# A two-block transformer kernel: parts of the branch outputs by blocks, one branch piece moved ahead of the last turn, merges moved ahead of the output weights' splits

## The reference, cut to what matters

```python
def hybrid_layer(x, c_act, ...):
    ...
    proj = h @ w_in
    pool_u, pool_g, q, k, v, ret_g, rw, rw_g, gate_logits = split(proj)
    o_pool = causal_pool_mixer(pool_u, pool_w, pool_scale) * silu(pool_g)
    o_ret = retention(q, k, v, positions, ret_norm_g) * silu(ret_g)
    o_rwkv = rwkv7_time_mix(rw, ...) * silu(rw_g)
    branches = stack([o_pool, o_ret, o_rwkv], axis=2)
    y = einsum('btnw,nwd->btnd', branches, w_branch)      # 3 x (512 -> 1024)
    gates = sigmoid(gate_logits.reshape(B, T, 3, D))
    merged = sum(gates * y, axis=2)
    return x + gate * (merged @ w_out)                    # 1024 -> 1024
```

## Time and profile before

| | before |
|---|---|
| median of 3 runs | 1726.67 us (1725.91 to 1729.78) |
| the profiled execution's own time | 1726.03 us |
| its span, first to last instruction | 1724.2 us |
| mean granted clock of TensorE over the span | 0.993 |
| PE busy | 1671.1 us (97%), 15204 matmuls |
| DVE busy | 1011.1 us (59%) |
| ACT busy | 718.6 us (42%) |
| POOL busy | 613.2 us (36%) |
| chain that ended last | PE 84%, DVE 7%, ACT 4%, POOL 4% |

### The profile page before, as it was taken

How to read it: one execution, slowest core, us unless ns; L and a number is a source line. 1 busy time by engine, 2 the same in 40 slices (tenths; PEclk the granted TensorE clock), 3 DMA queues, 4 the chain that set the end, 5 groups by cost and what they waited for, 6 DMA issues and landing times.

```text
span 1724.2 us, 34425 instructions
## 1 busy us (share of the span) xinstructions
PE 1671.1 (97%) x15204; PEld 1532.7 (89%) x15204; DVE 1011.1 (59%) x1620; ACT 718.6 (42%) x1120; POOL 613.2 (36%) x498
## 2 busy tenths in 40 slices
PE   9999999999999999999999999999999999999997
PEld 8888988899989888987999898999998898999986
DVE  4265366877763554476777776663344767643346
ACT  4444534545345444444444454532222544332323
POOL 1744673000307635733000304325545016154541
PEclk9999999999999999999999999999999999999999
DMA  8422444777545413465776544433223454332322
GB/s 347 148 99 74 147 172 197 275 277 265 175 175 189 139 63 119 135 268 196 272 271 213 184 171 142 165 123 124 99 99 123 147 171 143 139 124 99 124 75 110
DMA packets 44148, 283.57 MB, mean 164 GB/s; under 512 B 5160, under 2 KB 5288, under 8 KB 14176
## 3 DMA queue, kind: packets, MB, share of 16 engines
q1 hardware_dynamic: 42336, 272.23, 44.4%
q0 software_dynamic: 1664, 9.15, 1.4%
HBM read 280.30 MB, written 1.06 MB: 163 GB/s over the span
## 4 chain that ended last, share of the span: by engine, by line
PE 84%; DVE 7%; ACT 4%; POOL 4%; issue 1%; POOLq 0%; ACTq 0%; DVEq 0%
PE ps L532 81%; PE ps L540 3%; POOL part0l L2777 2%; POOL part1l L2777 1%; ACT Xh L2293 1%; DVE part0l L1284 1%; DVE gates L2026 1%; DVE part1l L1284 1%; ACT part0h L2293 1%; ACT part1h L2293 1%; DVE Xl L1299 0%; ACT Z L2290 0%; ACT gates L2290 0%; DVE small L1315 0%; DVE QK L1658 0%
## 5 line engine op out<-in xcount | busy, mean ns | idle before, releaser
L2293 ACT ACTIVATE part0h<-ring 128x1024 fp32r<-128x1024 f32 (+2 forms) x218 | 216.5, 1042 | 261.2 <-PE ps L532 253.7
L532 PE MATMUL ps<-Xh,part0h 128*128 128x256 f32 x1080 | 313.6, 290 | 5.1 <-DVE Xl L1299 3.3
L2293 ACT ACTIVATE part1h<-ring 128x1024 fp32r<-128x1024 f32 x218 | 216.5, 1041 | 231.9 <-PE ps L532 230.5
L532 PE MATMUL ps<-Xl,part0h 128*128 128x256 f32 x1080 | 306.0, 283 | 0.0
L532 PE MATMUL ps<-Xh,part0l 128*128 128x256 f32 x1080 | 305.8, 283 | 0.0
L532 PE MATMUL ps<-Xh,part1h 128*128 128x256 f32 x984 | 285.4, 290 | 2.0 <-DVE Xl L1934 1.8
L2777 POOL TENSOR_TENSOR part1l<-ring,part1h 128x512 fp32r<-128x512 f32 x172 | 222.8, 1327 | 159.2 <-ACT part1h L2293 159.2
L532 PE MATMUL ps<-Xl,part1h 128*128 128x256 f32 x984 | 279.0, 283 | 0.0
L532 PE MATMUL ps<-Xh,part1l 128*128 128x256 f32 x984 | 278.7, 283 | 0.0
L2777 POOL TENSOR_TENSOR part0l<-ring,part0h 128x512 fp32r<-128x512 f32 x164 | 216.0, 1350 | 155.0 <-ACT part0h L2293 154.8
L532 PEld LDWEIGHTS ps<-Xh,part0h 128*128 128x128 f32 x1080 | 207.2, 192 | 14.9 <-DVE Xl L1299 5.5
(11 more groups left out here) (410 smaller groups left out, 3322.1 us busy)
## 6 DMA issues: line engine op xcount, KB each, us to landing
ring<-in_w SPq DMA_DIRECT2D x214, 1024.0 KB, 4.9
hid<-in_ada SPq DMA_DIRECT2D x36, 512.0 KB, 6.0
hid<-in_w SPq DMA_DIRECT2D x6, 1024.0 KB, 10.2
rows<-in_lnrow POOLq DMA_DIRECT2D x6, 1024.0 KB, 8.1
fqk<-in_ada SPq DMA_DIRECT2D x6, 512.0 KB, 6.1
cq<-in_ada SPq DMA_DIRECT2D x6, 512.0 KB, 5.8
gates<-in_c SPq DMA_DIRECT2D x2, 1536.0 KB, 6.5
plain<-in_w SPq DMA_DIRECT2D x2, 1024.0 KB, 7.2
```

Source lines behind the costliest of these rows:

```text
L532: return e.matmul(o, a, b, start=st, stop=sp)
L2293: return e.activation(o, a, ACT.Copy)
```

## The change

It has four parts:

- `jobs2()` had bw1_0.1 and bw1_1.0 in one group; now each of the eight jobs is a group, and TensorE calls `jobs.fill()` once more, ahead of `turn_y(l, 1)`. The other engines' programs have no such call there, and so do the same job after the turn, in `jobs.rest()`, as before.
- The `pr` job writes the parts in four steps of two blocks (512 columns) in place of two steps of four blocks (1024 columns), on ACT and on DVE, each with a signal of its own.
- On DVE the merges 0 and 1 of branch 2 come ahead of out0's low part, merges 2 and 3 ahead of out1's.
- On ACT the high parts of merged quarters 0 and 1 come ahead of out0's split, those of quarters 2 and 3 ahead of out1's.

```diff
@@ -453,7 +453,7 @@
     halves = [f"h{b}_{j}.{m}" for b in range(3) for j in range(4) for m in range(2)]
     bw = [f"bw{b}_{hf}.{m}" for b in range(2) for hf in range(2) for m in range(2)]
     first += [halves[0:2]] + [[n] for n in halves[2:14]] + [halves[14:16]]
-    return first + [halves[16:18]] + [[n] for n in halves[18:24] + ["pr"] + bw[0:5]] + [bw[5:7], bw[7:8]]
+    return first + [halves[16:18]] + [[n] for n in halves[18:24] + ["pr"] + bw]
@@ -1255,6 +1255,7 @@
         for i in range(2):
             chunk(l, i, jobs)
+        jobs.fill()
         turn_y(l, 1)
@@ -1929,11 +1930,12 @@
         elif name == "pr":
-            for n, src, k in (("P", M.sgP, 0), ("R", M.sgR, 4)):
-                w.wait_ge(*at["PRhi", n, l])
-                e.tensor_tensor(X[1][:, k:k + 4, :], src, f32(X[0][:, k:k + 4, :]), ALU.subtract).then_inc(
-                    *V("PR", l, k // 2))
-                V.mark("PR", l, k // 2 + 1)
+            for n, src in ((0, M.sgP), (1, M.sgR)):
+                for q in range(2):
+                    k = 4 * n + 2 * q
+                    w.wait_ge(*at["PRhi", k // 2, l])
+                    e.tensor_tensor(X[1][:, k:k + 2, :], src[:, 2 * q:2 * q + 2, :], f32(X[0][:, k:k + 2, :]),
+                                    ALU.subtract).then_inc(*V("PR", l, k // 2))
@@ -2260,9 +2262,9 @@
         for j in range(4):
-            if j % 2 == 0:
-                use(l, f"bw2_{j // 2}")
             merge(l, 2, j)
+            if j % 2:
+                split_to(PIECE[l, f"out{j // 2}"])
         for j in range(4):
             use(l, f"out{j}")
@@ -2636,9 +2638,11 @@
         elif name == "pr":
             w.wait_ge(*done["X read", l])
             w.wait_ge(*at["oP", l])
-            copy(X[0][:, 0:4, :], M.sgP).then_inc(*S("PRhi", "P", l))
+            for q in range(2):
+                copy(X[0][:, 2 * q:2 * q + 2, :], M.sgP[:, 2 * q:2 * q + 2, :]).then_inc(*S("PRhi", q, l))
             w.wait_ge(*at["oR", l])
-            copy(X[0][:, 4:8, :], M.sgR).then_inc(*S("PRhi", "R", l))
+            for q in range(2):
+                copy(X[0][:, 4 + 2 * q:6 + 2 * q, :], M.sgR[:, 2 * q:2 * q + 2, :]).then_inc(*S("PRhi", 2 + q, l))
@@ -2748,11 +2752,12 @@
         for hf in range(2):
-            use(l, f"bw2_{hf}")
+            split_to(PIECE[l, f"bw2_{hf}"])
             for j in (2 * hf, 2 * hf + 1):
                 w.wait_ge(*at["merged2", 2, j, l])
                 w.wait_ge(*done["PR read", l])
                 copy(X[0][:, 2 * j:2 * j + 2, :], v(M.mgx[j], c=2, n=256)).then_inc(*S("mghi2", l, j))
+            split_to(PIECE[l, f"out{hf}"])
```

## The result

| | before | after |
|---|---|---|
| median, 20 runs each on the same chips | 1728.21 us (1725.91 to 1731.65) | 1732.26 us (1728.07 to 1734.88) |
| ratio | | 1.0022, 95% interval [1.0015, 1.0028] |
| the profiled execution | 1726.03 us | 1731.8 us |
| its span, mean granted clock | 1724.2 us, 0.993 | 1730.0 us, 0.990 |

The change makes the kernel slower, by a little over 0.2%. I had forecast 0.1% faster, and the time lies above my range. (The three runs shown before stood 1.5 us under the median of the twenty.)

What follows compares the result with a forecast made beforehand. TensorE, busy 97% of the span, was taken as the bound, with waits of 5.6 us a layer. Gains of 0.8 + 0.1 = 0.9 us a layer, 1.8 in all, gave a median of 1724.9 us, range 1721.5 to 1728.2.

Steps and rivals of the forecast that it cites:

- the forecast's sum: Whole kernel: gains of 0.8 + 0.1 = 0.9 us a layer, 1.8 us in all.
- the last rival: TensorE's clock falls behind the new waits at bw2_0 and out1, 1.75 us a fall, 1731.9 with four; chance 0.07.
- Part 1: At the `pr` job: parts written in smaller steps let bw0_0.0 start 1.17 us earlier; gain 0.8 us a layer.
- a subtraction of 512 takes DVE 0.69: At the `pr` job: the length taken for each of DVE's small steps, 0.69 us.
- Step W: TensorE's step behind DVE's masked key score copies: can begin at 1284.78, where it began at 1285.59.
- Part 2: At the turn: bw1_0.1 fills the wait, but POOL's wait at bw2_0 grows to 2.7 us; loss 0.57 us a layer.
- POOL's four steps: At bw2_0's low part: stretched beside three DVE merges, they take 5.98 us.
- the third rival: At bw2_0: each merge's sum holds POOL wholly, about 0.7 us, 7.1 in all; 1727.1 us; chance 0.12.
- Part 3: At the output product: out0's two waits go, out1 waits 1.3 us and starts 0.1 us earlier, Part 2's loss included.
- now merge 0 is over before bw2_0 ends: On DVE ahead of out0: merge 1 can start when bw2_0 ends, at 1326.39.
- the chain through merges 2 and 3: On DVE and ACT ahead of out1: its low part waits behind both merges, so TensorE starts out1 at 1338.9.

Runs made afterwards that it cites:

- e5: The changed kernel with 5 unread products ahead of bw2_0's first matmul on TensorE: 1728.14 us, ratio 1.0008 to the kernel before.
- e8: The kernel before with only the `pr` parts in four smaller steps (and groups of one job): 1727.89 us, ratio 0.9998.
- e2: The changed kernel without the extra `jobs.fill()` ahead of `turn_y(l, 1)`: 1727.23 us, ratio 1.0004 to the kernel before.
- e4: The changed kernel with bw2_0's split put ahead of `A0h` on ACT by one more `jobs.fill()`: 1723.69 us, ratio 0.9977 to the kernel before.
- e9: The changed kernel with, on ACT, bw2_0's split ahead of `A0h`; out1's parts ahead of merges 2 and 3; bw2_1's low part on DVE: 1720.45 us, ratio 0.9960.
- e7: The kernel before with only the merges moved ahead of the output splits on DVE and ACT: 1728.75 us, ratio 1.0010.
- e1: The kernel before with only the groups of one job and the extra `jobs.fill()` ahead of the turn: 1733.04 us, ratio 1.0035.
- e3: The changed kernel with 20 unread products ahead of bw2_0's first matmul on TensorE: 1740.85 us, ratio 1.0071 to the kernel before.

## Why the prediction was wrong

**The clock.** The first step that failed: the forecast's sum has no term for a fall of the clock, and the last rival, which got 0.07, is what happened, behind the wait at bw2_0 in both layers, though not behind the one at out1. Right in it were the mechanism and the wait that sets it off (2.7 us written, 2.39 found); its price of 1.75 us a fall measured 0.94 and 2.05. That its 1731.9 lies so near the measured 1732.26 is luck: it takes four falls, and two by its price give 1728.4.

Wrong was the chance. I took the earlier trace rows, where one wait of 1.8 us had a fall behind it and another of 1.6 none, as a sign that falls are rare. But the trace before, read over the whole run, has falls behind two of its four waits of 1.8 us (the one of the earlier trace rows and one that ends at 1425.92) and behind one of 1.65 us at 534.73; and I did not ask what a wait longer than any of these would do. Here are all waits of TensorE of 1.2 us or more in the eleven profiles of this study (the first and the last 20 us left out). The counts say behind how many of them a fall began, within the wait or up to 2 us after it:

| wait | at the second block's layer ends | elsewhere |
|---|---|---|
| 2.4 us | 4 of 4 | none there |
| 2.1 us | 2 of 4 | 11 of 12 |
| 1.9 us | 0 of 2 | none there |
| 1.8 us | 0 of 6 | 10 of 22 |
| 1.6 us | 0 of 8 | 3 of 11 |
| 1.2 to 1.3 us | 0 of 21 | 1 of 44 |

So a fall becomes likelier as the wait grows, no length up to 2.1 us decides it, and the counts differ from place to place, for a reason that no run here shows. Each profile also has one fall near 515 us that stands behind no wait of this length. The 20 runs of the changed kernel fit: the three at a mean clock of 0.993 took 1728.07 to 1729.27 us, as long as `e5`, the seven at 0.991 to 0.992 took 1730.46 to 1732.93, and the ten at 0.989 to 0.990 took 1731.8 to 1734.88. Shown is that filling the wait takes the falls at the layer ends away.

**Part 1** was to bring 0.8 us a layer and brought 0.18 at the turn and 0.20 at out2 (`e8`). The step that failed is "a subtraction of 512 takes DVE 0.69". DVE's timeline, the first two of the four steps, and POOL's last of bw0_0:

```profile
1281.03 1.32 DVE L1937 TENSOR_TENSOR Xl<-sg,Xh 128x512 fp32r<-128x512 f32 x1 [1.98 <-ACT Xh L2295]
1282.27 0.68 DVE L1937 TENSOR_TENSOR Xl<-sg,Xh 128x512 fp32r<-128x512 f32 x1
...
1280.54 1.27 POOL L2782 TENSOR_TENSOR part0l<-ring,part0h 128x512 fp32r<-128x512 f32 x1
```

DVE begins while POOL's step runs and is done 0.54 us behind POOL's end at 1281.81. Before, the larger step began only 0.35 us ahead of POOL's end. So most of the earlier start was given back. All four small steps end 4.04 us behind the zero, where the two large ones ended at 3.92, and the key score copies end at 6.60 for 6.49, where I had both 0.5 us earlier. Step W starts 0.2 us earlier all the same, because before it began 0.3 us later than the copies required.

**Part 2.** Right: the turn 1.23 us later (+31.84 against the +30.61 of `e2` or `e8`), `A0h` as the gate 2.72 us behind it, the split 0.53 behind that, POOL 1.13 on, and that the buffer's earlier release brings nothing; `e4` shows that the gate is `A0h`'s place in ACT's order. Mis-sized: POOL's four steps, 5.98 written and 6.36 found. One by one:

```profile
1316.34 1.30 POOL L2782 TENSOR_TENSOR part1l<-ring,part1h 128x512 fp32r<-128x512 f32 x1 [6.46 <-ACT part1h L2295]
1317.59 1.74 POOL L2782 TENSOR_TENSOR part1l<-ring,part1h 128x512 fp32r<-128x512 f32 x1
...
1316.67 1.51 DVE L1964 TENSOR_TENSOR sg<-sg,mt 128x512 f32<-128x512 f32 x1
1318.11 0.68 DVE L1960 SCALAR_TENSOR_TENSOR mt<-gates,ps 128x512 f32<-128x512 f32 x1
1318.82 1.06 DVE L1964 TENSOR_TENSOR sg<-sg,mt 128x512 f32<-128x512 f32 x1
```

Each POOL step behind such an overlap takes 1.71 to 1.74 us for some 1.27, and each DVE sum (two inputs in SBUF) 1.06 to 1.51 for 0.69; the merge's other half, whose product comes from PSUM, keeps its 0.68. The Trainium skill, page "SBUF — State Buffer", section "Who interferes with whom", says that a DVE instruction with two SBUF inputs and a POOL instruction that reads SBUF contend, that one with at most one SBUF input does not, and that the port pair they share is "an exclusive lock". The trace agrees with all three. POOL's first step, which began alone, takes 1.30 and ends at 1317.64, the sum that began within it ends at 1318.18, 0.54 later, and POOL's next step is 0.47 longer. The next two sums end 0.55 behind the POOL steps that ran when they began (1319.33 and 1321.03). So the third rival had the kind right, and its price was too high: a sum holds POOL for 0.47 us, not for the 0.7 of its shown duration, and three add 1.4 us to 4.94. The trace before had that price, hidden in the 5.59 for four steps:

```profile
1317.47 1.74 POOL L2777 TENSOR_TENSOR part1l<-ring,part1h 128x512 fp32r<-128x512 f32 x1
```

**Part 3.** Right: no wait at out0 (the falls don't change that), and a new one at out1, by the chain through merges 2 and 3. That it was 1.3 us, as written, is luck: without the fall, which made TensorE later at out1, it is 1.91 (`e5`). The step that failed is "now merge 0 is over before bw2_0 ends". In `e5`, where no fall blurs it, merge 1 starts 0.6 us behind bw2_0's end:

```profile
1325.86 0.69 DVE L1961 SCALAR_TENSOR_TENSOR mt<-gates,ps 128x512 f32<-128x512 f32 x1 [3.61 <-PE ps L532]
1326.58 1.10 DVE L1965 TENSOR_TENSOR sg<-sg,mt 128x512 f32<-128x512 f32 x1
1328.39 1.01 DVE L1301 TENSOR_TENSOR Xl<-sg,Xh 128x512 fp32r<-128x512 f32 x1 [0.70 <-ACT Xh L2296]
1329.32 0.67 DVE L1961 SCALAR_TENSOR_TENSOR mt<-gates,ps 128x512 f32<-128x512 f32 x1
```

The durations of the earlier trace rows that I used are those of a time when POOL is idle. Moved ahead of out0's split, merge 0 lies beside POOL's low part of bw2_1, and its two steps with two SBUF inputs, the sum and the low part, take 0.7 us more. In `e9` POOL has no low part to make there, and merge 0's sum takes 0.69 again:

```profile
1326.32 0.69 DVE L1964 TENSOR_TENSOR sg<-sg,mt 128x512 f32<-128x512 f32 x1
```

Part 3 by itself is 0.35 us late at out2 in layer 0 (`e7`), where I had it about 0.7 early.

**The sum.** Without falls I had -0.9 us a layer; `e5` gives +0.65. The 1.55 between them are 0.6 of part 1, 0.4 of POOL's steps and 0.6 of merge 0, with one cause in all three: a DVE step with two SBUF inputs beside a POOL step. For merge 0 `e9` shows it by taking POOL's step away; for the other two it is read from the rows. The falls and these terms failed by about as much. Twice 1.55, the 3.0 of the falls and the 1.5 by which the shown median stood low make 7.6, and 1732.26 - 1724.9 is 7.4.

## What to carry to other kernels

Where TensorE is busy 97% of the time, price a wait by what comes behind it: several short waits may be cheaper than one of their sum (5.6 us a layer before, 5.4 in the changed kernel), and the list of waits doesn't show the difference, only the granted clock behind each does. When a step is moved, take its duration from a row in which its new neighbours run too, on both engines. And before work is moved ahead on one engine, look in what order the others do what it waits for: part 2 became a gain (1.0022 to 0.9977) only when ACT's order was changed with it.

## What I had not expected of the hardware

- A fall of the clock ahead of another wait is partly or wholly free: 1.54 us lost at out0 in the changed kernel were 0.94 at out2. Between layer 0's out2 and layer 1's zero, where the program is the same in all eleven, seven profiles have a fall behind a wait of 1.8 us, and the next wait, 8 us on, is 0.7 to 0.8 us for 2.1; the stretch takes 295.40 to 295.44 us. The changed kernel's profile has no fall there and takes 295.42. The other three (`e1`, `e3`, `e9`) have the fall behind the second wait and take 296.87 to 296.93. So the same 3.4 us at half clock cost nothing or 1.5 us, by whether a wait followed. That second wait before and in the changed kernel:

```profile
1434.26 0.38 PE L532 MATMUL ps<-part0h,Xh 128*128 128x256 f32 x1 [0.75 <-DVE part0l L1284]
...
1437.31 0.39 PE L532 MATMUL ps<-part0h,Xh 128*128 128x256 f32 x1 [2.10 <-DVE part0l L1285]
```

- An fp32 product of 256 columns by 128 x 128 numbers took 0.42 us (two records of 0.21) in `e3`, where one of the shorter format takes 0.12 ahead of the wait in the changed kernel.
- The stretch at half clock isn't of one length: in the changed kernel it is 3.4 us in layer 0 and 6.8 in layer 1 behind waits of 2.39 and 2.38 us, from the same program text. What decides it no run here shows.
